# Expert stage of a three-block model: first weight halves split ahead, router with tokens moving, batched choice of experts, last sums by column half

## The reference, cut to what matters

```python
D_MODEL, SEQ, N_EXPERTS, TOP_K, D_FF_EXPERT = 1024, 256, 8, 2, 3584

def swiglu(h, w_gate, w_up, w_down):
    return (jax.nn.silu(h @ w_gate) * (h @ w_up)) @ w_down

def moe_swiglu(h, router, we_gate, we_up, we_down):
    logits = (h @ router).astype(jnp.float32)
    top_v, top_i = lax.top_k(logits, TOP_K)
    top_w = jax.nn.softmax(top_v, axis=-1)
    gates = jnp.sum(jax.nn.one_hot(top_i, N_EXPERTS, dtype=jnp.float32) * top_w[..., None], axis=-2)
    out = jnp.zeros_like(h)
    for e in range(N_EXPERTS):
        out = out + gates[..., e:e + 1] * swiglu(h, we_gate[e], we_up[e], we_down[e])
    return out
# h = h + moe_swiglu(rms_norm_3(h, sw_ffn_norm_g), ...)
```

## Time and profile before

| | us |
|---|---|
| median of 3 runs | 2342.98 (2341.79 to 2345.45) |
| the profiled execution, its time | 2341.53 |
| its span | 2339.7 |
| busy PE / DVE / ACT in the span | 2156.7 / 1549.0 / 1238.1 |

### The profile page before, as it was taken

How to read it: one execution, slowest core, us unless ns; L and a number is a source line. 1 busy time by engine, 2 the same in 40 slices (tenths; PEclk the granted TensorE clock), 3 DMA queues, 4 the chain that set the end, 5 groups by cost and what they waited for, 6 DMA issues and landing times.

```text
span 2339.7 us, 30150 instructions
## 1 busy us (share of the span) xinstructions
PE 2156.7 (92%) x10510; PEld 1750.3 (75%) x10510; DVE 1549.0 (66%) x2085; ACT 1238.1 (53%) x1601; POOL 19.1 (1%) x33
## 2 busy tenths in 40 slices
PE   5799897886799999899999799999999999999998
PEld 4568664674499977699865688888888888888886
DVE  3342314456556657555434798989899898989896
ACT  0103210344444344544324587878787787878785
POOL 0000000000000000000100000000000000000000
PEclk9799879897899999999999799999999999999999
DMA  8764223431365431555431499989999898989894
GB/s 309 218 249 144 90 90 126 153 126 37 127 197 180 144 110 53 180 181 185 130 108 55 152 362 334 367 332 370 361 334 381 312 381 319 386 322 370 328 369 156
DMA packets 270558, 534.04 MB, mean 228 GB/s; under 512 B 29060, under 2 KB 80781, under 8 KB 270349
## 3 DMA queue, kind: packets, MB, share of 16 engines
q1 hardware_dynamic: 257808, 522.42, 62.4%
q10 hardware_dynamic: 11821, 7.38, 1.3%
q0 software_dynamic: 848, 3.15, 0.4%
HBM read 529.77 MB, written 3.14 MB: 228 GB/s over the span
## 4 chain that ended last, share of the span: by engine, by line
PE 86%; DVE 7%; ACT 3%; issue 2%; DMA 1%; SPq 0%; ACTq 0%; POOL 0%; DVEq 0%
PE sum L1418 13%; PE bank L686 9%; PE bank L1400 9%; PE bank L1402 9%; PE bank L1401 9%; PE sum L1075 6%; PE sum L747 5%; PE bank L1090 3%; PE bank L1091 3%; PE bank L1092 3%; PE bank L1349 1%; PE bank L702 1%; PE bank L827 1%; PE sum L1179 1%; PE bank L1388 1%
## 5 line engine op out<-in xcount | busy, mean ns | idle before, releaser
L2626 DVE TENSOR_TENSOR x_lo<-ring,x_hi 128x1024 fp32r<-128x1024 f32 x672 | 779.6, 1220 | 57.1 <-ACT x_hi L1881 41.4
L1881 ACT ACTIVATE x_hi<-ring 128x1024 fp32r<-128x1024 f32 x672 | 694.9, 1059 | 140.2 <-PE bank L1402 81.2
L1400 PE MATMUL bank<-x_hi,hg_hi 128*128 128x512 f32 x896 | 355.5, 397 | 4.8 <-DVE x_lo L2626 4.8
L1402 PE MATMUL bank<-x_hi,hg_lo 128*128 128x512 f32 x896 | 350.5, 391 | 0.0
L1401 PE MATMUL bank<-x_lo,hg_hi 128*128 128x512 f32 x896 | 349.8, 390 | 0.0
L686 PE MATMUL bank<-hT,ring 128*128 128x256 f32 x1024 | 238.6, 396 | 20.9 <-issue 9.3
L686 PEld LDWEIGHTS bank<-hT,ring 128*128 128x128 f32 x1024 | 203.1, 200 | 55.4 <-issue 16.8
L2066 DVE TENSOR_TENSOR w_lo<-ring,w_hi 128x1024 fp32r<-128x1024 f32 x130 | 157.9, 1225 | 124.0 <-ACT w_hi L1707 122.3
L1707 ACT ACTIVATE w_hi<-ring 128x1024 fp32r<-128x1024 f32 x130 | 136.9, 1061 | 150.2 <-PE bank L1092 80.3
L1400 PEld LDWEIGHTS bank<-x_hi,hg_hi 128*128 128x128 f32 x896 | 169.0, 189 | 38.4 <-DVE x_lo L2626 5.2
L1402 PEld LDWEIGHTS bank<-x_hi,hg_lo 128*128 128x128 f32 x896 | 168.9, 188 | 36.3
(11 more groups left out here) (420 smaller groups left out, 2793.2 us busy)
## 6 DMA issues: line engine op xcount, KB each, us to landing
ring<-in_sw_we_gate SPq DMA_DIRECT2D x112, 1024.0 KB, 7.1
ring<-in_sw_we_up SPq DMA_DIRECT2D x112, 1024.0 KB, 7.1
ring<-in_sw_we_down SPq DMA_DIRECT2D x112, 1024.0 KB, 7.2
ring<-in_w_in SPq DMA_DIRECT2D x36, 1024.0 KB, 5.1
ring<-in_w_ff SPq DMA_DIRECT2D x32, 1024.0 KB, 5.4
ring<-in_ada_w SPq DMA_DIRECT2D x24, 1024.0 KB, 7.2
ring<-in_w_out SPq DMA_DIRECT2D x12, 1024.0 KB, 4.9
ring<-in_cv_w_gate SPq DMA_DIRECT2D x11, 1024.0 KB, 5.2
```

Source lines behind the costliest of these rows:

```text
L1400: mm(ps[b][:, :], hg_hi[:, k, :], hi[:, cols], start=(k == 0), stop=False)
L1402: last = mm(ps[b][:, :], hg_lo[:, k, :], hi[:, cols], start=False, stop=(k == KC - 1))
L1881: go(f(x_hi[:, hp % MSLOTS, :], ring[:, s, lo:lo + PIECE // 2], ACT.Copy), c.sig("hi_ready", hp))
L2626: v.tensor_tensor(x_lo[:, hp % MSLOTS, :], ring[:, s, lo:lo + PIECE // 2], x_hi[:, hp % MSLOTS, :].bitcast(F32), ALU.subtract).then_inc(c. ...
```

## The change

- `AHEAD = 3`: halves 0 to 2 of round 0 are split by ACT and DVE at the end of the attention loop; those of every later round at the end of the round before (`high_next`, `low(..., next_)`), two of them ahead of the last `act_high`/`act_low`, one behind. SP loads the two pieces that this needs once more after the last round.
- ACT makes one root (a table load) behind the first splits and one exponential ahead of the router's.
- Tile 0 of `nrm` gets its gain row inside `norm_x` (`widen_gain`), after PE has turned it (`tile_turned`).
- The router has `rw` as weights (8 columns) and `hT` moving (256 columns): 8 matmuls. ACT copies the 8x256 result, PE turns it back with two small transposes.
- `keep_busy(n)` issues n matmuls of 128x128 by 256 columns into `acc[0]`: 3 between the turned tiles, 4 after the logits.
- The choice of experts is made for both tiles in one instruction each; `PG` is gone, the gates reach PE as `gsel`; constants are set before the norm; the first dispatch stands ahead of the gates. The zero matmuls are gone.
- PE waits for the two halves of the gathered tokens one by one.
- `narrow_last` does all of `acc[0]` and then all of `acc[1]`, starting with `act_hi` and waiting for `act_lo` after 8 matmuls. Behind the loop `ey_hi`, `ey_lo`, scatter, additions and stores go by column half, four stores of 256 KB.

```diff
-                    sp.wait_ge(*(c.at if i >= 0 else c.before)("lo_ready", hp))
+                    sp.wait_ge(*(c.at if i >= 0 and hp >= AHEAD else c.before)("lo_ready", hp))
...
+                c.loop = n_rounds
+                expert(0, ROUND_PIECES[:(AHEAD + 1) // 2])
...
+            for h in range(2):
+                for t in range(NT):
+                    sp.wait_ge(*c.at("x_ready", h, t))
+                    sp.dma_start(out.rearrange("a (t p) d -> p (a t) d", p=P)[:, t, h * 512:(h + 1) * 512],
+                                 xres[:, t, h * 512:(h + 1) * 512]).then_inc(c.sem("out_stored"), 16)
...
+            def keep_busy(n):
+
+                for _ in range(n):
+                    mm(acc[0][:, 0:S], ident, C("upto", 2)[:, 0, :], start=True, stop=True)
...
+                if t == 0:
+                    last.then_inc(c.sig("tile_turned").sem, 1)
+                    keep_busy(3)
             pe.wait_ge(c.sem("rw_in"), 16)
             b = J.fill(pe, "router")
+            for k in range(KC):
+                if k % 2 == 0:
+                    pe.wait_ge(*J.emptied("moe", k // 2))
+                last = mm(ps[b][0:NEXP, 0:S], rw[:, k, :], hT[:, k, :], start=(k == 0), stop=(k == KC - 1))
+            done(last, "router")
+            b = J.fill(pe, "logits")
...
-            done(last, "router")
+                last = nc.tensor.transpose(ps[b][:, t * 8:t * 8 + 8], aT[0:NEXP, t * P:(t + 1) * P], ident[0:NEXP, 0:NEXP])
+            done(last, "logits")
+            keep_busy(4)
             pe.wait_ge(*c.at("selected"))
...
+                        if key == "xg" and g == 0 and q % 2 == 0:
+                            pe.wait_ge(*c.before("gathered", "next", q // 2))
...
+                def narrow_last(g):
+
+                    ks = range(4 * g, 4 * g + 4)
+                    pe.wait_ge(*c.at("act_high", g))
+                    w = {}
+                    for k in ks:
+                        w[k] = split(2 * ROUND_PIECES.index(("xdown", k // 2)) + k % 2)
+                        for x in w[k]:
+                            mm(acc[0][:, :], act_hi[:, k % 8, :], x[:, 0:512], start=False, stop=False)
+                    pe.wait_ge(*J.emptied("xt", g))
+                    for k in ks:
+                        last = mm(acc[0][:, :], act_lo[:, k % 8, :], w[k][0][:, 0:512], start=False, stop=(k == ks[-1]))
+                    last.then_inc(c.sig("half_summed").sem, 1)
+                    for k in ks:
+                        hp = 2 * ROUND_PIECES.index(("xdown", k // 2)) + k % 2
+                        mm(acc[1][:, :], act_hi[:, k % 8, :], w[k][0][:, 512:D], start=False, stop=False)
+                        mm(acc[1][:, :], act_hi[:, k % 8, :], w[k][1][:, 512:D], start=False, stop=False)
+                        last = mm(acc[1][:, :], act_lo[:, k % 8, :], w[k][0][:, 512:D], start=False, stop=(k == ks[-1]))
+                        s = c.sig("piece_used", "xdown", k)
+                        last.then_inc(s.sem, 1)
+                        W.half_free(hp, s)
...
-                narrow(GROUPS - 1)
+                narrow_last(GROUPS - 1)
...
+            for h in range(2):
+                pe.wait_ge(*c.at("ey_low_end", h))
+                for t in range(NT):
+                    scatter(t, h, (acc[2 + h], ps[h])[t]).then_inc(c.sig("scattered_end", h, t).sem, 1)
...
 
+            for hp in range(AHEAD):
+                if hp % 2 == 0:
+                    act.wait_ge(*W.ready(ROUND_PIECES[hp // 2]))
+                s, lo = W.place(ROUND_PIECES[hp // 2]), (hp % 2) * (PIECE // 2)
+                go(f(x_hi[:, hp, :], ring[:, s, lo:lo + PIECE // 2], ACT.Copy), c.sig("hi_ready", "first", hp))
+            do(f(aT[:, 510:511], ones[:, 0:1], ACT.Sqrt))
             roots("moe", 0, 1)
...
+                def high_next(upto):
+
+                    for hp in range(next_[0], upto):
+                        if hp % 2 == 0:
+                            act.wait_ge(*W.landed(ROUND_PIECES[hp // 2], ahead=1))
+                        act.wait_ge(*W.half_wait(hp, ahead=1))
+                        s, lo = W.place(ROUND_PIECES[hp // 2]), (hp % 2) * (PIECE // 2)
+                        go(f(x_hi[:, hp % MSLOTS, :], ring[:, s, lo:lo + PIECE // 2], ACT.Copy), c.sig("hi_ready", hp))
+                    next_[0] = upto
 
...
                 act_high(GROUPS - 1)
+                high_next(AHEAD)
                 c.leave()
...
-                do(f(ey_hi[:, h * 512:(h + 1) * 512], acc[h][:, :], ACT.Copy, scale=gcol[:, 0:1]), c.sig("ey_high_end") if h else None)
+                act.wait_ge(*(c.at("piece_used", "xdown", FFE // P - 1) if h else c.at("half_summed")))
+                do(f(ey_hi[:, h * 512:(h + 1) * 512], acc[h][:, :], ACT.Copy, scale=gcol[:, 0:1]), c.sig("ey_high_end", h))
             c.loop = None
...
+            def widen_gain():
+
+                dve.wait_ge(c.sem("moe_gain_in"), 16)
+                dve.wait_ge(*c.at("tile_turned"))
+                do(v.tensor_tensor(nrm[:, 0, :], nrm[:, 0, :], wide[:, :], ALU.mult))
...
+                if i == SW_PAIRS + SM_PAIRS + 1:
+                    for hp in range(AHEAD):
+                        dve.wait_ge(*c.at("hi_ready", "first", hp))
+                        s, lo = W.place(ROUND_PIECES[hp // 2]), (hp % 2) * (PIECE // 2)
+                        v.tensor_tensor(x_lo[:, hp, :], ring[:, s, lo:lo + PIECE // 2],
+                                        x_hi[:, hp, :].bitcast(F32), ALU.subtract).then_inc(c.sig("lo_ready", "first", hp).sem, 1)
...
+            do(v.tensor_tensor(nrm[:, 1, :], nrm[:, 1, :], wide[:, :], ALU.mult))
...
+            do(v.tensor_copy(flat(l), bank("logits")[:, 0:16]), J.free("logits"))
+            do(v.tensor_tensor(above, others, mine, ALU.is_gt))
+            do(v.tensor_tensor(below, others, mine, ALU.is_equal))
+            do(v.tensor_tensor(below, below, lower, ALU.mult))
+            do(v.tensor_tensor(above, above, below, ALU.add))
+            do(v.tensor_reduce(rt[:, 3, :, :], above, AX, ALU.add))
+            do(v.tensor_scalar(flat(rt[:, 1, :, :]), flat(rt[:, 3, :, :]), 2.0, None, ALU.is_lt), c.sig("selected"))
+            do(v.tensor_reduce(xtr[:, 0:NT, 0], l, AX, ALU.max, negate=True), c.sig("router_max"))
             do(v.tensor_copy(pos[:, 1, :, 0:NEXP], rt[:, 1, :, :]))
-            for t in range(NT):
-                do(v.tensor_scalar(pos[:, 2, t, 0:NEXP], rt[:, 4, t, :], xtr[:, t, 2:3], None, ALU.mult))
+            do(v.tensor_scalar(pmT[:, :], C("upto", 2)[:, 0, :], 0.0, None, ALU.mult))
+            do(v.memset(gcol[:, :], 0.0))
...
-                for m, a in ((Pm, 1), (PG, 2)):
-                    for t in range(NT):
-                        do(v.tensor_scalar(m[:, t, :], C("iota"), pos[:, 0, t, at_], pos[:, a, t, at_], ALU.is_equal, ALU.mult),
-                           c.sig("dispatch_ready", key) if a == 2 and t else None)
+                for t in range(NT):
+                    do(v.tensor_scalar(Pm[:, t, :], C("iota"), pos[:, 0, t, at_], pos[:, 1, t, at_], ALU.is_equal, ALU.mult),
+                       c.sig("dispatch_ready", key) if t else None)
...
+            def select_gate(at_):
+
+                do(v.tensor_copy(gsel[:, 0:NT], pos[:, 2, :, at_].rearrange("p t a -> p (t a)")))
...
+                    do(v.tensor_copy(xtr[:, 6, 3:4], ones[:, 0:1]), c.sig("gathered", key, q))
+
+            b = bank("slots")
+            do(v.tensor_copy(pos[:, 0, :, 0:NEXP], b[:, 0:16].rearrange("p (t e) -> p t e", t=NT)))
             dispatch(slice(0, 1), "first")
...
+            do(v.tensor_copy(count, b[:, 16:24]), J.free("slots"))
+            dve.wait_ge(*c.at("exp_done", "router"))
+            do(v.tensor_tensor(flat(rt[:, 4, :, :]), flat(rt[:, 2, :, :]), flat(rt[:, 1, :, :]), ALU.mult))
+            do(v.tensor_reduce(xtr[:, 0:NT, 1], rt[:, 4, :, :], AX, ALU.add))
+            do(v.reciprocal(xtr[:, 0:NT, 2], xtr[:, 0:NT, 1]))
+            do(v.tensor_tensor(pos[:, 2, :, 0:NEXP], rt[:, 4, :, :], spread(xtr[:, 0:NT, 2], 8), ALU.mult))
+            select_gate(slice(0, 1))
...
+            do(v.tensor_copy(ridi[:, :], rid[:, :]), c.sig("rounds_ready"))
+            do(v.tensor_tensor(hit, axes(one, [0, 3 * NT], one.ap[1], one.ap[2]),
+                               axes(table, table.ap[1], [0, EXTRA], [1, 8]), ALU.mult))
+            do(v.tensor_reduce(table[:, :, NEXP:NEXP + EXTRA], hit, AX, ALU.add))
...
+                        select_gate(bass.ds(r + 1, 1))
                         dispatch(bass.ds(r + 1, 1), "next")
                 low(HALVES - 1)
                 gathered("next")
                 low(HALVES)
```

More of the change, by code:

```diff
@@ L78 @@
 MSLOTS = 7
+AHEAD = 3
 SPLITS = 6
@@ L255, in half_free, with half_wait @@
         self.halves[hp] = (signal.name, signal.base)
-    def half_wait(self, hp):
+    def half_wait(self, hp, ahead=0):
         name, v = self.known.halves[(hp - MSLOTS) % HALVES] if self.known else ("piece_used", 1)
-        if hp < MSLOTS and self.known:
```

(50 more changed lines are left out.)

119 lines of the change are left out of this document (43 added, 76 removed).

## The result

| | before | after |
|---|---|---|
| median (range) of 4 runs each, side by side, us | 2342.78 (2341.79 to 2345.45) | 2322.06 (2321.37 to 2324.88) |
| ratio | | 0.9912, 95% interval 0.9895 to 0.9929 |
| profiled execution, its time / span, us | 2341.53 / 2339.7 | 2324.88 / 2323.1 |
| stretch from the mark to the end, us | 1059.15 | 1037.81 |

The account below looks back on a forecast made before the run. The prediction took TensorE (PE) to bound the expert rounds, with DVE the second limit at 90%. Gains of 5.8 + 13.0 + 4.3 = 23.1 us gave a 2318.4 us profiled execution, a median of about 2320.0; range 2316.5 to 2327.5.

Parts of the forecast that it names:

- A: In each expert round: PE's stall on `act_lo` shrinks, 0.72 us sooner eight times, 5.8 us; bounds 0 and 11.9.
- C: Behind the last round: work by column half ends the span 7.2 us after the last product, saving 4.3 us.
- B: Stretch ahead of the rounds, norm to first scatter: 13.7 us saved at full clock, 5.7 at half; 13.0 taken.
- R2: Rival, in the rounds: moved splits hold `act_high` back, so the stall gain is nothing; 2325.8 us, chance 0.09.
- Step 1: Norm, ahead of the router: the root's table load is made early; 0.7 us counted.
- step 2: Router: 8 products of 256 columns take 3.8 us at full clock, 7.7 at half, against 6.98 before.
- Step 3: Logits' way back after the router: copy, two transposes, two waits delay the choice by 1.2 us; bounds 0.7, 1.7.
- step 6: Gather, up to the end of the second `hg_hi`: 5.50 to 3.57 us at full clock; saves 1.9, or 0.
- Step 7: End of second `hg_hi` (G) to first scatter: splitting ahead saves 4.45 us, with a new `ey_low` wait of about 2.4.
- R1: Rival: the clock stays low up to the gather, total gain 15.8 us, time 2327.2 us; chance 0.18.
- R3: Rival, slower: next expert's first piece is late, PE stands idle at each round's end; 2347.9 us, chance 0.03.
- R4: Rival: change does less, `ey_low` wait eats the gain before the first scatter, stores no faster; 2325.7 us, chance 0.09.

Follow-up runs that it names:

- x_plain_narrow: Changed kernel with the last group done by the old `narrow` instead of `narrow_last`, halves still split ahead; 2327.38 us.
- x_no_ahead: Changed kernel with `AHEAD = 0` instead of 3, so no half is split ahead, before the loop or in the rounds; 2326.79 us.
- x_more_fill: Changed kernel with more filler matmuls: 4 instead of 3 between the turned tiles, 2 ahead of the router, 2 behind the slots; 2317.13 us.
- x_old_tail: Changed kernel with only the part behind the last round undone: by token tile, two stores of 512 KB; 2321.17 us.
- x_fill_front: Changed kernel with fillers only ahead of the router: 4 between the turned tiles, 2 before the router's products, none later; 2318.71 us.
- x_no_fill: Changed kernel without its seven filler matmuls (3 between the turned tiles, 4 after the logits); 2320.66 us.
- x_old_router: Changed kernel with the router as before: `hT` as weights, `rw` moving, no copy and no turning back; 2324.37 us.
- x_early_ey: Changed kernel with ACT and DVE making the scaled sums `ey_hi` and `ey_lo` after half 3 instead of half 5; 2319.89 us.
- x_early_turn: Changed kernel with the last group's activation turned, and split, ahead of the narrow of the group before; 2310.26 us.

## Why the prediction was right

It forecast 2320.0 us; 2322.06 were measured, inside its range. A and C came out as forecast in size, B 1.8 us short.

**A: right.** 5.8 forecast; from the first scatter to the recorded end of the last product it is 998.66 before (1059.15 - 49.02 - 11.47) and 993.04 after (1037.81 - 37.80 - 6.97), 5.6 less. PE starts 0.13 behind `act_hi`, the wait is 0.76 eight times, a round 124.8. The moved splits did not hold `act_high` back (R2): ACT took it up 0.73 us after it became idle, waiting for PE's turn. The 0.72 a round was booked to the new order. It takes the splits ahead as well: without the order the round is 125.5 (x_plain_narrow), without the splits 125.4 (x_no_ahead), because PE then comes to the first scatter before `ey_lo` is done. The prediction had `ey_lo` come 1.6 us sooner, which is what keeps that wait away, but it gave no price for it.

**B: the mechanism right, two terms mis-sized.** By steps, from the marks (before to after):

| step | forecast | measured | from |
|---|---|---|---|
| 1 norm | 0.7 | 0.6 at the turn of tile 1, 0.26 at the router | 10.90 to 10.28; 12.60 to 12.34 |
| 2 router | 3.2 (-0.7 at half) | 1.7 | 6.96 to 5.30 long |
| 3 way back | -1.2 | -0.5 | 0.69 to 1.19 |
| 4 choice | 1.15 | 1.16 | 2.96 to 1.80 |
| 5 to the gather | 3.5 (2.4) | 3.8 | 6.25 to 2.44 |
| 6 gather to G | 1.9 (0) | 0.2 | 6.20 to 5.98 |
| 7 G to scatter | 4.45 | 4.6 | 13.36 to 8.75 |
| sum | 13.7, taken 13.0 | 11.2 | 49.02 to 37.80 |

- The step that failed is the clock, in 2 and 6: "three matmuls (1.3 us) fill most of that". They filled it and did not hold the clock. It fell to 0.50 at the router and again at the gather, so half of step 2 and nearly all of step 6 were missing: 3.2 us, as much as x_more_fill gives back. R1 was half right: it had the clock low through all of both, and it was low in the first part of each. The term should have been taken between full and half for each stage, not near full for both.
- Step 3 was a slip that hid part of this: the earlier trace rows have 0.67 us between the router's end and the choice before the change, and I counted the whole new way of 1.2 as if the old had been nothing. At full clock throughout the scatter comes 14.4 sooner (x_more_fill: 49.02 - 34.63), not 13.7. So the slip made good about 0.7 us of what the clock took, and that part of B's nearness is luck; without it the forecast would have been 2319.3, its range as it was.
- Step 1: the turn of tile 1 came 0.62 sooner, but DVE's first `hT` follows it by 0.92 instead of 0.55 us. In x_no_ahead this 0.37 is absent. Why the splits ahead cost it is open; the trace shows DVE waiting for nothing there.
- Step 7 is the part that mattered most and it held: the scatter is set by DVE at G + 8.7, whether PE starts its products before G (28.30) or behind it (26.39 against 25.90 in x_more_fill). The forecast wait of 2.4 was 2.16, plus one on `x_lo` of 1.3 that I had not named; both lie inside the time that DVE takes anyway and add nothing to the sum.

**C: right.** E + 7.2 forecast, E + 6.97 measured (E is the last product's recorded end, 2315.73 + 0.40, and the span ends at 2323.1). The additions end at E + 4.46, as worked; the last store took 2.0 us to land instead of 2.4. x_old_tail puts it back at 11.5.

**R3** (a late piece) did not come: no wait on the ring stands among PE's in the rounds. **R4**: `ey_lo` does wait, but within step 7's sum.

The Trainium skill, "TensorE: Matmul & The Clock Gate", Part 1, has idleness return TensorE to half rate and sustained matmul activity release it. The runs agree with the first half in part: the clock is 0.50 after PE stood 0.84 and 0.89 us around the turned tile 1 (the changed kernel), after 2.17 us of waiting for the choice (x_fill_front), and in the tail, where PE stood 3.16 us (x_old_tail), and it stays 1.00 through router and gather with all twelve fillers (x_more_fill). But x_no_ahead has waits of 0.84 and 0.52 us around the tile and stays at 1.00. With the second half the runs agree for the new router, and not for the old form, which was busy 6.82 of 6.82 us and stayed at 0.51.

What stays open: why x_no_ahead kept the full clock with the seven fillers that did nothing in the changed kernel. Its router began 0.37 us sooner, so PE stood 0.84 and 0.52 us ahead of it instead of 0.84 and 0.89; the changed kernel's clock fell 12.5 us behind the mark, when its router had run for 0.16 us, and that of x_no_ahead had then run for 0.53. That this gap decides was not tried by itself. x_no_fill stood 2.14 and 0.89 us, and its clock fell at the same place as the changed kernel's. Behind the router the waits of x_no_ahead (0.61, 0.24 and 1.10 us) are those of the changed kernel (0.61, 0.25 and 1.10), whose clock fell again ahead of the gather.

## What to carry to other kernels

Before trusting work that is to keep the clock up, run the kernel once without it: seven fillers changed nothing, twelve were worth 3.2 us, and six ahead of the router did not keep the clock up for the gather. Where a wait of the bounding engine comes from its own product's way through two others, issue that product one step earlier (early turn: 8.5 us, where the waits' row said 6.1), rather than only shortening the wait. Moving an engine's step forward pays only where that engine is not the bound afterwards. Here the early sums came 2.1 us sooner and cost 1.9 in the same round.

## What the runs showed of the hardware

- A wait of PE costs more than its row says. The 0.76 us on `act_hi` cost 1.04 to 1.06 a round: without it the next matmul starts before the recorded end of the one ahead (starts 0.23 apart at 0.39 recorded), and the first after a wait is followed only 0.33 us later instead of 0.23.
- The two forms of the router's product met the fallen clock differently. With 8 moving columns against 128 weight columns it stayed at 0.51 for 6.8 us (x_old_router). With 256 moving columns against 8 weight columns it went from 0.50 to 1.00 within the router (5.30 us in all, 3.61 at full clock).
- The clock's changes went with the work. In the changed kernel, x_no_fill, x_plain_narrow, x_old_tail, x_early_ey and x_early_turn it fell 12.5 us behind the mark, came back at 15.9, fell at 22.7 and came back at 26.1, though their marks lie up to 8.3 us apart.
- Thirteen traces, of before, after and the eleven experiments, put the mark up to 8.3 us apart; from the mark on two kernels that differ only in fillers that do nothing (the changed kernel and x_no_fill) agree within 0.1 us. A difference of 2 us between two kernels of 2320 us is better read from the mark than from medians, as long as the edit lies behind the mark.
